# Modulation vectors of a transformer stack: a layer's own gate joins its jobs, at most six a layer, folded at other steps

## The reference

```python
mod = jnp.split(c_act @ w_ada[l] + b_ada[l], N_MOD, axis=-1)
h = modulate(rms_norm(x, ffn1_norm[l]), mod[0], mod[1])
x = x + FFN_RESIDUAL * (1 + mod[2])[:, None, :] * swiglu(h, ffn1_w_gu[l], ffn1_w_down[l])
...
def modulate(h, shift, scale):
    return h * (1 + scale[:, None, :]) + shift[:, None, :]
def swiglu(h, w_gu, w_down):
    g, u = jnp.split(h @ w_gu, 2, axis=-1)
    return (jax.nn.silu(g) * u) @ w_down
...
# second stack: the same with mod_w, six vectors a block, and
# conv_ffn: a causal convolution of width 3 on the gate half, then gelu
```

## Time and profile before

| | |
|---|---|
| median of 3 runs | 3518.0 us (3516.31 to 3521.98) |
| the profiled execution | 3515.23 us |
| its span in the trace | 3513.4 us |
| TensorE matmul busy | 3268.3 us, 93% |
| VectorE busy | 1943.5 us, 55% |
| GpSimd busy | 1007.1 us, 29% |
| ScalarE busy | 1195.6 us, 34% |

### The profile page before, as it was taken

The page is one execution under the profiler, slowest core; times in us unless marked ns, Lnnn a source line. Parts: engine busy times, 40 slices in busy tenths (PEclk is TensorE's granted clock), DMA queues, the critical chain, the costliest instruction groups (busy, mean ns, idle before and its releaser), DMA issues.

```text
span 3513.4 us, 40734 instructions
## 1 busy us (share of the span) xinstructions
PE 3268.3 (93%) x14517; PEld 2599.4 (74%) x14517; DVE 1943.5 (55%) x2837; ACT 1195.6 (34%) x1803; POOL 1007.1 (29%) x713
## 2 busy tenths in 40 slices
PE   6998999999999999998999989988999978599998
PEld 4886876678777888775788777757878857478887
DVE  5656455656545533555655443347675479764443
ACT  3222243532223222335422223354333233143332
POOL 2888000068803800000188500001884021000000
PEclk9999999999999999999999999989999999699999
DMA  6665352156634633331366433202664332023332
GB/s 205 197 197 176 94 136 62 38 176 196 186 93 137 191 96 96 85 86 31 96 197 198 149 90 108 72 1 90 200 194 145 95 103 73 13 84 92 99 92 88
DMA packets 577202, 417.69 MB, mean 119 GB/s; under 512 B 30123, under 2 KB 537370, under 8 KB 575942
## 3 DMA queue, kind: packets, MB, share of 16 engines
q1 hardware_dynamic: 532434, 283.99, 27.4%
q0 software_dynamic: 34304, 121.64, 11.6%
q10 hardware_dynamic: 10356, 10.69, 1.0%
HBM read 408.91 MB, written 6.06 MB: 118 GB/s over the span
## 4 chain that ended last, share of the span: by engine, by line
PE 60%; POOL 15%; DVE 15%; issue 4%; ACT 3%; DMA 2%; ACTq 0%; SPq 0%; DVEq 0%; POOLq 0%
PE bank L324 17%; PE bank L326 17%; PE bank L325 17%; POOL mod_acc L674 8%; POOL mod_w L671 4%; PE bank L1276 2%; PE bank L1307 2%; DVE tmp L449 2%; POOL mod_w L643 2%; DMA mod_w<-in_w_ada 2%; DVE w_lo L305 2%; DVE h_lo L459 1%; POOL mod_acc L677 1%; PE bank L1297 1%; DVE w_lo L296 1%
## 5 line engine op out<-in xcount | busy, mean ns | idle before, releaser
L324 PE MATMUL bank<-h_hi,w_hi 128*128 128x512 f32 x2656 | 1052.9, 396 | 69.4 <-DVE w_lo L305 24.0
L325 PE MATMUL bank<-h_lo,w_hi 128*128 128x512 f32 x2656 | 1042.1, 392 | 0.0
L326 PE MATMUL bank<-h_hi,w_lo 128*128 128x512 f32 x2656 | 1041.9, 392 | 0.0
L305 DVE TENSOR_TENSOR w_lo<-raw,w_hi 128x1024 fp32r<-128x1024 f32 x438 | 655.1, 1496 | 536.2 <-ACT w_hi L288 534.3
L288 ACT ACTIVATE w_hi<-raw 128x1024 fp32r<-128x1024 f32 x438 | 462.1, 1055 | 663.5 <-PE bank L326 661.0
L324 PEld LDWEIGHTS bank<-h_hi,w_hi 128*128 128x128 f32 x2656 | 502.5, 189 | 203.9 <-issue 48.8
L326 PEld LDWEIGHTS bank<-h_hi,w_lo 128*128 128x128 f32 x2656 | 502.3, 189 | 107.6
L325 PEld LDWEIGHTS bank<-h_lo,w_hi 128*128 128x128 f32 x2656 | 503.0, 189 | 102.9 <-issue 0.2
L674 POOL TENSOR_TENSOR mod_acc<-mod_acc,mod_w 128x1024 f32<-128x1024 f32 x168 | 457.2, 2721 | 14.0
L324 PE MATMUL bank<-hid_hi,w_hi 128*128 128x512 f32 x1056 | 414.6, 393 | 16.4 <-DVE w_lo L305 16.3
L326 PE MATMUL bank<-hid_hi,w_lo 128*128 128x512 f32 x1056 | 413.1, 391 | 0.0
(11 more groups left out here) (313 smaller groups left out, 3336.5 us busy)
## 6 DMA issues: line engine op xcount, KB each, us to landing
raw<-in_ffn_w_gu SPq DMA_DIRECT2D x176, 512.0 KB, 3.9
mod_w<-in_w_ada POOLq DMA_DIRECT2D x128, 512.0 KB, 4.0
mod_w<-in_mod_w POOLq DMA_DIRECT2D x96, 512.0 KB, 4.2
raw<-in_ffn_w_in SPq DMA_DIRECT2D x88, 512.0 KB, 3.7
raw<-in_ffn_w_down SPq DMA_DIRECT2D x64, 512.0 KB, 3.5
raw<-in_w_in SPq DMA_DIRECT2D x34, 512.0 KB, 3.7
raw<-in_ffn_w_out SPq DMA_DIRECT2D x32, 512.0 KB, 3.5
raw<-in_ffn_w_down SPq DMA_DIRECT2D x32, 384.0 KB, 3.1
```

The costliest lines, as they stand in the source:

```text
L305: loop(nc.vector.tensor_tensor(w_lo[:, u % 2, :], raw[:, u % 2, :], w_hi[:, u % 2, :].bitcast(F32), ALU.subtract), "split_lo", times)
L324: nc.tensor.matmul(dst, a_hi, b_hi, start=start, stop=False)
L325: nc.tensor.matmul(dst, a_hi, b_lo, start=False, stop=False)
L326: return nc.tensor.matmul(dst, a_lo, b_hi, start=False, stop=stop)
```

## The change

`mod_jobs` gets a rule in place of its table. Each feed-forward layer makes its own gate first, then of the next two sublayers shift and scale if that is a feed-forward layer, and all three if it is a mixer (unless an earlier layer made them). The lists become: layer 0 own gate, all of 1, two of 2 (six vectors); layer 2 own gate, two of 3, all of 4 (six); layer 3 own gate, two of 5 (three); layer 5 own gate, all of 6, two of 7 (six); layer 7 own gate, all of 8, two of 9 (six); layer 9 own gate (one). There are again 28. All folds are now in the first half, after steps 6, 9, 13, 16, 19 and 21. The third sublayer of a list is spread and turned into columns in pass 3 of the second half, the first two in `after_hidden`. `mod_sums` becomes a call per phase, so that layer 9's vector comes behind GpSimd's work for mixer 8.

```diff
-        FOLD_AT = [6, 9, 12, 15, 18, 21]
+        FOLD_AT = [6, 9, 13, 16, 19, 21]
 
         def mod_jobs(key):
 
-            if key[0] != "f" or key == final:
+            if key[0] != "f":
                 return []
             n = ORDER.index(key[1])
-            if n == 0:
-                return [(0, 2)] + [(t, j) for t in (ORDER[1], ORDER[2]) for j in range(3)]
-            ahead = {("f", 2): (1, 2), ("f", 3): (2,), ("f", 5): (1, 2), ("f", 7): (1, 2)}[key]
-            return [(ORDER[n + k], j) for k in ahead for j in range(3)]
+            jobs = [(ORDER[n], 2)]
+            for t in (n + 1, n + 2):
+                kind = [k for k, s in PHASES if k != "b" and t < len(ORDER) and s == ORDER[t]]
+                if kind == ["f"]:
+                    jobs += [(ORDER[t], 0), (ORDER[t], 1)]
+                elif kind and not (t == n + 1 and n and ("f", ORDER[n - 1]) in PHASES):
+                    jobs += [(ORDER[t], j) for j in range(3)]
+            return jobs
...
+        def set_parts(key, s):
+            return [j for t, j in mod_jobs(key) if t == s]
...
             def body(i, times):
-                if isinstance(i, int) and len(mod_jobs(key)) > 3:
-                    mod_spread(pe, key, mod_jobs(key)[-1][0], 7)
+                if isinstance(i, int) and len(mod_sets(key)) > 2:
+                    mod_spread(pe, key, mod_sets(key)[2], 7)
...
-                if isinstance(i, int) and i == 2 and len(jobs) > 3:
-                    mod_fold(dve, key, len(jobs) - 1)
-                if isinstance(i, int) and i == 3 and len(jobs) > 3:
-                    mod_coef(dve, jobs[-1][0], [0, 1, 2], 7)
+                if isinstance(i, int) and i == 3 and len(sets) > 2:
+                    mod_coef(dve, sets[2], set_parts(key, sets[2]), 7)
...
-            folding = FOLD_AT[:len(jobs) - (len(jobs) > 3)]
+            folding = FOLD_AT[:len(mod_jobs(key))]
...
-            mod_sums(pool)
+            mod_begin(pool)
             for key in PHASES:
+                mod_sums(pool, key)
                 if key[0] == "o":
                     pool_odd(pool, key)
...
                 def after_hidden(dve):
-                    sets = mod_sets(key)
-                    if key == PHASES[0]:
-                        mod_coef(dve, 0, [2], 4)
-                        mod_coef(dve, sets[1], [0, 1, 2], 7)
-                    elif sets:
-                        mod_coef(dve, sets[0], [0, 1, 2], 4)
+                    for s, bank in zip(mod_sets(key)[:2], (4, 7)):
+                        mod_coef(dve, s, set_parts(key, s), bank)
```

More of the change, by code:

```diff
@@ L246, in emit @@
             pe = act = dve = sp = 0
-            norms = adds = 0
+            norms = adds = vectors = 0
             sq_act = sq_dve = 0
         turn = Turn()
+        turn.former = {}
         total = known.get("units", 1 << 30)
@@ L634, in gate_of, with mod_begin, mod_sums @@
             return lambda m: coef[:, ORDER.index(s) % 3, bass.ds(m + 16, 1)]
-        def mod_sums(pool):
+        def mod_begin(pool):
             wait(pool, "act_c", "c")
             pool.wait_ge(sg.sem(f"mod0_loaded{KT - 1}"), 16)
+        def mod_sums(pool, key):
             def fetch(src, slot):
                 pool.dma_start(mod_w[:, slot, :], src).then_inc(sg.sem(f"mod_loaded{slot}"), 16)
[L646 to L671, removed]
-                        pool.wait_ge(sg.sem("mod_step"), sg.count["mod_step"])
[L673 to L680, removed]
@@ new lines, in mod_sums, with src @@
+            for n, (s, j) in enumerate(mod_jobs(key)):
+                if n == 0:
+                    wait(pool, "norm_lo", (key, KT - 1))
+                name, l, part = SETS[s]
+                c0 = 0 if name == "w_ada" else KT
+                acc = mod_acc[:, j * D:(j + 1) * D]
+                def src(t):
+                    return d[name][l, t * P:(t + 1) * P, (3 * part + j) * D:(3 * part + j + 1) * D]
+                fetch(src(0), 0)
+                if j in turn.former:
+                    wait(pool, "mod_folded", turn.former[j])
+                turn.former[j] = (s, j)
+                for t in range(KT):
+                    if t + 1 < KT:
+                        fetch(src(t + 1), (t + 1) % 2)
+                    pool.wait_ge(sg.sem(f"mod_loaded{t % 2}"), 16 * (4 * turn.vectors + t // 2 + 1))
+                    w, c = mod_w[:, t % 2, :], cact[:, c0 + t:c0 + t + 1]
+                    if t == 0:
+                        done(pool.tensor_scalar(acc, w, c, 1.0, ALU.mult, ALU.mult), "mod_step")
+                        pool.wait_ge(sg.sem("mod_step"), sg.count["mod_step"])
+                        continue
+                    done(pool.tensor_scalar(w, w, c, 1.0, ALU.mult, ALU.mult), "mod_step")
+                    pool.wait_ge(sg.sem("mod_step"), sg.count["mod_step"])
+                    if t < KT - 1:
+                        done(pool.tensor_tensor(acc, acc, w, ALU.add), "mod_step")
+                        pool.wait_ge(sg.sem("mod_step"), sg.count["mod_step"])
+                    else:
+                        done(pool.tensor_tensor(acc, acc, w, ALU.add), "mod_summed", (s, j))
+                wait(pool, "mod_summed", (s, j))
+                turn.vectors += 1
@@ L957, in body @@
                             fold_shift(dve, nxt, u0 + 4 * per)
-            repeat(dve, 4, body, last=True, alone=(2,) if len(jobs) > 3 else ())
+            repeat(dve, 4, body, last=True)
             turn.dve += 4 * per
@@ L2638, in after_hidden @@
                 def after_hidden(pe):
[L2639 to L2643 removed]
+                    for s, bank in zip(mod_sets(key)[:2], (4, 7)):
+                        mod_spread(pe, key, s, bank)
                 if key[0] == "f":
```

8 lines of the change are left out of this document (1 added, 7 removed).

## The result

The changed kernel takes 3530.07 us in the median of six runs (3525.42 to 3533.69), the kernel before took 3519.61 us in six runs (3511.96 to 3521.98). The ratio is 1.0031, with a 95% interval of 1.0018 to 1.0044: some 11 us slower. The prediction had said 3536, in a range of 3525 to 3546, and slower with a chance of 90%. Sign, range and mechanism hold; the size came out at some 11 of the 18 us.

A forecast was written before the change was run, and what follows sets the result against it. TensorE, busy 93% of the span, was taken to bound the kernel, so only its idle or slow-clock time counts. Terms summed to 17.7, so 18 us: 3515.2 to 3533 profiled, 3536 us median, range 3525 to 3546.

The forecast's parts named there:

- mechanism: Seams bound by GpSimd in layers 2 and 5 and a disturbed layer 9: 3525 to 3542 us, chance 78%.
- The late sums: Layers 2 and 5: GpSimd's sixth sum ends at 967.1 and 1984.6, before at 967.97 and 1987.25, after TensorE's first half.
- From sum to output: Seams of layers 2 and 5: from the sixth sum's end to the second half's first output takes 13.4 us.
- In layer 2, +2.5 for +4.2: Layer 2: the sixth fold waits for GpSimd after step 21, first output at 980.5 instead of 976.32, +4.2 us.
- In layer 5, +12.8 for +11.3: Layer 5: same wait where the seam had no loss before, first output at 1998.0 instead of 1986.68, +11.3 us.
- Layer 0: Layer 0: wait at step 21 stays; without the seventh vector GpSimd's work leaves the second half, gaining 5.8 us.
- Layer 9: Start of layer 9: a vector summed beside the first steps delays w_lo as in layer 7, +6.5 us.
- Layer 7: Layer 7: the sixth fold comes to the seam with its sum ready; 0.6 us late, taken as +1.
- The sum: Whole kernel: -5.8 + 4.2 + 11.3 + 1 + 6.5 + 0.5 = 17.7, so 18 us slower.
- the rival in which GpSimd keeps pace: All three fold waits go because six sums take less than TensorE's first half: -13 us, 3505 us, chance 3%.
- The time that layer 2 gains by the removed wait doesn't count: Layer 2: removing the 7.13 us wait after step 18 gains nothing, since GpSimd sets the end.

The follow-up runs named there:

- experiment 1: Changed kernel with the sixth fold of layers 0, 2, 5 and 7 moved back to pass 2 of the second half; 3502.36 us, ratio 0.9966 to the kernel before.
- experiment 3: Changed kernel with one more vector summed by GpSimd at the end of layer 0's list and folded nowhere; 3532.59 us, ratio 1.0053 to the kernel before.
- Experiment 4: Changed kernel with GpSimd's vector of layer 9 begun only when three hid_lo of that layer are written; 3520.49 us, ratio 1.0025 to the kernel before.
- experiment 7: Changed kernel with seven of eight products and the seven adds of layer 9's vector on 8 columns only; 3528.64 us, ratio 1.0018 to the kernel before.
- experiment 2: Changed kernel with the old fold steps 6, 9, 12, 15, 18, 21, all six in the first half; 3527.65 us, ratio 1.0045 to the kernel before.
- experiment 6: Kernel before with only the new fold steps 6, 9, 13, 16, 19, 21; 3505.88 us, ratio 0.9959 to the kernel before.
- experiment 5: Experiment 1 with GpSimd's lists in layers 7 and 9 begun only when two hid_lo are written; 3500.49 us, ratio 0.9944 to the kernel before.
- experiment 8: Experiment 1 with GpSimd's vector in layer 9 alone begun only when two hid_lo are written; 3499.39 us, ratio 0.9944 to the kernel before.
- experiment 9: Kernel before with new fold steps, at most five folds per first half, layer 0's last two in passes 1 and 2; 3498.79 us, ratio 0.9935.

## Why the prediction was right

**The late sums (right).** The prediction rested on GpSimd ending the sixth sum after TensorE has left the first half. The three waits of the profile after, and their disappearance in experiment 1, show it. Relative to the start of its layer the sum ended 1.25 us earlier in layer 2 than before (0.9 predicted) and 1.5 us earlier in layer 5 (2.6 predicted): the adds do become short while VectorE stands (2.34 us), but in layer 5 that saved less than I had taken: of the seven adds of this sum four took 3.24 to 3.26 us after, and three took 3.23 to 3.26 before.

**From sum to output (right in size).** 13.4 us were predicted. Measured: 962.53 to 974.64, 12.1 us in layer 2, and 1983.51 to 1997.24, 13.7 us in layer 5. The piece ahead of TensorE's restart took 5.77 and 6.18 us, where 6.8 had been read in layer 0, and the piece behind it 6.34 and 7.55, about the two ends that I had averaged. So the mean of the two was near, 12.9. In layer 2, +2.5 for +4.2, 1.3 of the 1.7 us lie in this piece. In layer 5, +12.8 for +11.3, only 0.3 us do, and 1.2 are the sum that ended later than forecast.

**Layer 0 (right, and another 2.7 us by chance).** The seventh vector was priced at 5.8 us from two spacings; the second half became 5.7 us shorter, and putting a vector back cost 6.6 in experiment 3. The first output came 2.7 us earlier as well, which no step had foreseen. The sixth sum ended at 308.41 + 2.40 = 310.81 in place of 312.87. Experiment 3 has the same code up to there and shows the output another 5 us earlier, so this is no effect that I can put down to an edit.

**Layer 9 (right).** +6.1 for +6.5, with the very wait and the very `w_lo` of layer 7 (4.15 and 3.37 us). That the wait agrees to 0.01 us is luck: the same instructions gave 4.94 to 5.02 us in experiments 1 to 3, with 248.8 to 249.6 us for the stage. Experiment 4 shows that it is GpSimd beside the first steps, experiment 7 that it is mostly its arithmetic.

**Layer 7 (mis-sized by 2.7 us).** +1 was predicted, -1.7 measured. The piece that the prediction spoke of, from the start of the last product `hid` of the first half to the first output, went from 12.12 to 12.90 us, +0.8. The rest is the layer's start, where five kernels with the same instructions gave 257.4 to 259.9 us.

**The sum.** So the terms that the change owns (-5.7, +2.5, +0.6, +12.8, +0.8, +6.1) make 17.1, against 17.7. The medians show 10.5, with an interval of 6 to 15 us by the ratio. Between the two stand pieces that no edit owns: -2.7 in layer 0, -2.5 at layer 7's start and +3.4 outside the stages make 15.3, the difference of the spans; and the profiled execution of before (3515.23) lies 4.4 us below the median of its six runs, while that of the changed kernel is at its median, so 10.9. A sum made against a single profile of before inherits both. So of the 7.2 us between 17.7 and 10.5, 0.6 are the terms' own, 1.8 the pieces that no edit owns, and 4.8 the distance of the two profiles from their medians. (One sum of the prediction is slightly off and changes nothing: the terms of the rival in which GpSimd keeps pace make -12.3, not -13.)

**The step that was true but misleading.** "The time that layer 2 gains by the removed wait doesn't count" holds for this change (experiment 2), but experiment 6 shows that these distances are worth 14 us in the kernel before, more than the removed wait with its gap. The prediction had the two gaps of layer 2 and the slow matmuls (its first rival prices them) but didn't ask what the kernel would be with the distances alone.

## What to carry to other kernels

When a consumer on the critical engine's supplier (here VectorE's fold) is put closer to its producer, compare the producer's end with the moment at which the critical engine passes that place; if it is later, the whole remainder goes onto the path, with the pipeline's refill and the slow clock behind it. A wait amid a loop and the same wait at a seam have different prices: 7.13 us of VectorE's waiting cost 2.98 us of idle TensorE amid the steps of layer 2 before, and 5.65 us at the seam of layer 0 after. So a fold belongs where its sum is ready, as in pass 2 of experiment 1. And take a change of several edits apart: here one gained 14 us and another lost more, and the fastest kernels (experiments 5, 8 and 9) keep the first and leave out the second.

## What the runs showed of the hardware that I had not expected

- VectorE's instructions on 8 columns can be as dear as large ones. At the seam of layer 7 in experiment 5 those that read a bank (of PSUM, the memory that TensorE writes to) took 0.15 and 0.17 us, the second of them beside a GpSimd add; those of the form `coef<-coef` took 1.45 and 2.24 us, until GpSimd's instruction ended, and 0.17 us in experiment 1, where GpSimd was done. The Trainium skill's page "SBUF — State Buffer", section "Who interferes with whom", says that a `tensor_scalar` can enter a mode that contends with GpSimd, and that the other fully blocks; the ends of the two rows agree with that (0.04 and 0.03 us behind GpSimd's). The start of the first does not fit as well: its row begins 0.28 us ahead of GpSimd's product, and 0.17 us would have been enough to be done before it. What holds it back that early is open.
- Which instruction meets which differs from kernel to kernel where the instructions are the same. The seam of layer 5 with no fold in it has no gap of over 1.7 us in experiment 1, one of 4.29 in experiment 8 and one of 4.21 in experiment 5, which have the same instructions there; the first wait of layer 7 was 3.51 us in the changed kernel and 5.29 to 5.53 in experiments 3, 4 and 7, with GpSimd's start not moved. What sets it was not tried, and stays open. It bounds what one profile can say of a stage.
- The price of a gap in TensorE is not in proportion to its length. In the 4 us behind gaps of 12.25 and 12.91 us ten matmuls were done, at a granted clock of 0.55 and 0.50; behind the gap of 3.75 us before, nine at 0.50. Gaps of 5.65 us (layer 0, after) and 5.43 us (experiment 5) also restart with matmuls of 0.80 and 0.79 us. And of the two gaps of 2.98 us in the kernel before, one was followed by 11 matmuls at 0.62, the other by 18 at 1.00.
- The untouched mixers vary between profiled executions too. Mixer 4 took 202.8 us from its start to its first output in experiment 2, 206.3 in the kernel before and 211.1 in experiment 7. Why is open.
